# Layer 0's u table is split into half-precision parts ahead of the choosing stage and kept in DRAM

## The chip, the core and the metric

The kernel runs on one core of a Trainium2 chip. The core has a matrix engine (PE, with a separate weight load, PEld), a vector engine (DVE), a scalar engine (ACT), a general engine (POOL, which also issues the indirect DMAs), a queue engine that only issues DMAs (SP), and 16 DMA engines that all queues share. Each engine runs its own program in order; they meet only at semaphores. The metric is the device time of one execution in microseconds (us); lower is better.

## The reference

The reference is a two-layer block on 512 tokens of width 1024 with 256 context tokens beside them (768 tokens in six tiles of 128 in layer 0). Layer 0 mixes tokens with latent attention and a gated linear attention, layer 1 with a gated recurrence; behind each stands a product-key expert layer ("PEER"), on which this change bears:

```python
q = (ht @ wq).reshape(n_tok, 8, 256)
s1, s2 = q[..., :128] . k1, q[..., 128:] . k2        # 128 scores each
t1, i1 = top_k(s1, 16);  t2, i2 = top_k(s2, 16)      # best of both halves
top_s, pos = top_k(t1 + t2, 16);  idx = the 16 pairs # of 128 * 128 experts
g = softmax(top_s)
act = gelu(einsum('td,thkd->thk', hb, u[idx]))       # u: 16384 x 1024 a layer
out = einsum('thk,thkd->td', g * act, v[idx])
```

## The kernel before

**Stages.** The kernel is a chain of blocks with a barrier behind each: `modulation_vectors`, `modulate_columns`, `project_l0` (14 projections of 128 columns, then a value product V of six tiles), `latent_norms`, `attention` (48 softmax steps), twice `gla_decays`, `gla_states`, `gla_outputs`, then `gla_norm_gate`, `project_and_norm`; then PEER for layer 0: `peer_scores` (16 query projections with their scores), `choose_and_activate`, `combine_with_dots`. Layer 1 follows with its mixer and the same PEER functions.

**The choosing stage.** `choose_and_activate` does not gather u for most tokens. It takes the table in 128 chunks of 128 experts (512 KB each in float32) and multiplies each chunk with all tokens of `nt` tiles (four in layer 0, three in layer 1; the remaining tiles are gathered, below), writes the GELU of every product to DRAM (`acts`), and makes a one-hot gate matrix for each tile (`gates`). float32 is reached by halves: a chunk is split into a float16 high part `uh` and a float16 low part `ul = u - uh`, and each product is three float16 matmuls (line 1483), 24 a chunk in layer 0.

**Who splits a chunk before.** SP loads the chunk into one of four buffers `ur`. ACT casts it to `uh` (L1514). For an odd chunk DVE subtracts (L1577). For an even chunk ACT also writes the negated chunk (L1516) and POOL issues a DMA that adds `ur` to it (L1444). `LOW_BY` holds this table, the same for both layers. PE waits for the low part.

**Order in the stage.** `schedule` is the order all engines follow: `pre` chunks (12 in layer 0, 16 in layer 1), then for each tile a *choices part* (`ahead` chunks, 12 or 17, beside which DVE finds the top sixteen of a tile; PE then turns the result, L1492) and a *gates part* (`beside` chunks, 16 or 19, between 16 gate steps: DVE builds one-hot blocks, L1721 to L1725, and PE multiplies them, L1502). The tile's exponentials on ACT (L1535) stand behind chunk 7 (layer 0) or 10 (layer 1) of a choices part, and DVE waits for them at L1690. The gathered tiles cost DVE one dot product per chosen row (L1607, 256 in layer 0, 128 in layer 1). POOL fetches their rows by indirect DMA (L1457) into four buffers `ug`/`HS`, each fetch waiting for the dot product four back. In layer 0, 32 dot products stand behind each choice and 40 in each gates part; the low parts of the chunks stand between them in DVE's program, and the L1444 issues between the fetches in POOL's.

**Other places the change touches.** In `project_l0` POOL cuts each weight block into halves (L258, L259) when PE has finished the block two before, and ACT copies each product out of PSUM (L294), two products at a time in flight. `peer_scores` is built likewise (L1206, L1207, L1242), with a store of the scores per projection from ACT's queue (L1245).

Of the kernel before, what the change touches and what calls it, by code (L numbers as in the profile page):

```python
# [15 lines left out]
F32 = mybir.dt.float32  # L16
# [7 lines left out]
P = 128  # L24
D = 1024
# [195 lines left out]
def project_l0(nc, io, hh, hl, PT, V):  # L221

    with ExitStack() as c:
# [10 lines left out]
        with signals(nc, "wv_in", "wv_high", "wv_cut", "v_prod", "v_copied", "w_in0", "w_in1", "w_cut", "prod", "copied",  # L234
                     "pown", "w_high") as (wv_in, wv_high, wv_cut, v_prod, v_copied, w_in0, w_in1, w_cut, prod, copied, pown, w_high):
            w_in = (w_in0, w_in1)

            with nc.Block() as block:
                @block.sync
                def _(sp):  # L240
                    with sp.Fori(0, N_PROJ // 2) as it:
                        for j in range(2):
                            sp.wait_ge(w_cut, it * 2 + (j + 1))
                            sp.dma_start(w[j][:, :, :], io["ev_w_in"][bass.ds(it * 2 + j, 1)].rearrange("o p (k m) -> p (o k) m", k=KD)).then_inc(w_in[j], 16)
# [40 lines left out]
                def _(act):  # L285
# [5 lines left out]
                    with act.Fori(0, N_PROJ // 2) as it:  # L291
                        for j in range(2):
                            act.wait_ge(prod, it * 2 + (j + 3))
                            nc.scalar.activation(PT[:, bass.ds(it * 2 + j, 1), :].rearrange("p o t -> p (o t)"),  # L294
                                                 ps[j][:, 0:TOK], ACT.Copy).then_inc(copied, 1)

                @block.vector
                def _(dve):
                    for j in range(2):
                        dve.wait_ge(w_high, j + 1)  # L300
                        nc.vector.tensor_tensor(wl[j][:, :, :], w[j][:, :, :], wh[j][:, :, :], ALU.subtract).then_inc(w_cut, 1)
                    dve.wait_ge(wv_in, 16)
# [79 lines left out]
def attention(nc, io, PT, MIX, ident, halves):  # L382
# [4 lines left out]
    with ExitStack() as c:  # L387
# [7 lines left out]
        for x in halves:  # L395
# [12 lines left out]
                 "exped", "normed", "turned", "pt_copied", "av_done", "out_copied", "own")  # L408
        with signals(nc, *names) as (cs_in, wv_in, w_in0, w_in1, q_done, k_done, v_done, q_copied, k_copied, v_copied, roped, score, maxed,
# [1997 lines left out]
```

## Time and profile before

| | us |
|---|---|
| median of 3 runs (4462.70 to 4464.65) | 4462.87 |
| the profiled execution | 4453.52 |
| its span | 4451.7 |
| `project_l0` in it | 146.2 |
| `peer_scores`, layer 0 | 152.9 |
| `choose_and_activate`, layer 0 / layer 1 | 1002.9 / 703.1 |
| PE busy over the span | 84% |
| DVE busy over the span | 68% |

The profiled execution is 9.4 us under the median; stages are read from it alone. A busy share is an average over stages with different limits, and pipelined matmuls overlap in their records, so each stage is read by itself: its length, and the wait that ends last in it. "A <- B: t, n, m" in a list of waits means that A stood idle t us in n pieces, the longest m, until B released it.

### The profile page before, as it was taken

What the parts mean: (1) busy time and instruction counts of PE and PEld (TensorE: products, weight loads), DVE (VectorE), ACT (ScalarE), POOL (GpSimd) and SP (SyncE); (2) the same over time, 40 slices, a digit from 0 to 9 for tenths busy, and PEclk for the clock granted to TensorE, in tenths of its full rate; (3) what the DMA queues carried; (4) which work ended last, traced back from release to release, by engine and by line L of the source; (5) the groups of instructions that cost most, each with busy time, mean ns of one, the idle gap of its engine ahead of it and who ended that gap; (6) DMA issues with size and microseconds to landing.
All of it is one profiled execution on the core that took longest, in us unless ns stands there. A gap on an engine that the chain in (4) does not pass through costs nothing. (4 is left out here: it accounts for less than half of the span.)

```text
span 4451.7 us, 59762 instructions
## 1 busy us (share of the span) xinstructions
PE 3746.2 (84%) x19545; PEld 1934.9 (43%) x19545; DVE 3039.8 (68%) x6128; ACT 1447.7 (33%) x1842; POOL 1623.1 (36%) x1253
## 2 busy tenths in 40 slices
PE   6998778988959595969999978877998787699996
PEld 1555663643424242424444423434555454344442
DVE  2036445157968696859999976853578686588887
ACT  0115220023424242422332314841354444333332
POOL 0400000311434342437777731202223324277774
PEclk8989878999979897989999989988999998899998
DMA  5200250346989898989999982122699998899995
GB/s 209 76 28 1 78 152 9 98 140 188 344 292 338 298 346 296 325 339 403 404 404 403 404 307 77 59 88 69 192 257 346 286 329 284 314 330 347 341 346 220
DMA packets 397431, 1086.93 MB, mean 244 GB/s; under 512 B 38000, under 2 KB 124848, under 8 KB 390576
## 3 DMA queue, kind: packets, MB, share of 16 engines
q1 hardware_dynamic: 204380, 505.65, 31.1%
q0 software_dynamic: 128448, 435.22, 30.3%
q10 hardware_dynamic: 64420, 143.77, 8.7%
q8 instruction: 97, 1.59, 0.1%
q14 instruction: 86, 0.70, 0.0%
HBM read 921.87 MB, written 130.12 MB: 236 GB/s over the span
## 5 line engine op out<-in xcount | busy, mean ns | idle before, releaser
L1483 PE MATMUL ca_A<-hh,ca_uh 128*128 128x512 f16 (+1 forms) x2048 | 747.8, 365 | 270.8 <-DVE ca_ul L1577 196.6
L1483 PE MATMUL ca_A<-hl,ca_uh 128*128 128x512 f16 (+1 forms) x2048 | 745.8, 364 | 0.0
L1483 PE MATMUL ca_A<-hh,ca_ul 128*128 128x512 f16 (+1 forms) x2048 | 745.1, 364 | 0.0
L1913 PE MATMUL ex_R<-ex_vl,hh 128*128 128x512 f16 x1792 | 682.8, 381 | 0.0
L1913 PE MATMUL ex_R<-hl,hh 128*128 128x512 f16 x1792 | 542.3, 381 | 78.4 <-DVE hh L1927 58.0
L1944 DVE SCALAR_TENSOR_TENSOR ex_sum<-ex_vg,ex_share,ex_sum 128x1024 f32<-128x1024 f32 x384 | 493.1, 1284 | 9.8 <-DVE ex_share L1936 6.0
L1457 POOL DMA_INDIRECT ca_ug<-in_peer_u_rows,chosen_rows x288 | 296.4, 1029 | 458.4 <-DVE ca_ug L1607 403.7
L1841 POOL DMA_INDIRECT ex_vg<-in_peer_v_rows,ex_index x384 | 376.8, 981 | 193.1 <-DVE ex_ar L1922 86.5
L1607 DVE SCALAR_TENSOR_TENSOR ca_ug<-ca_ug,ca_hp 128x1024 f32<-128x1024 f32 x288 | 346.2, 1217 | 125.7 <-DMA ca_ug<-in_peer_u_rows,chosen_rows 124.0
L1483 PEld LDWEIGHTS ca_A<-hh,ca_uh 128*128 128x128 f16 x2048 | 205.9, 101 | 477.3 <-DVE ca_ul L1577 210.5
L1524 ACT ACTIVATE ca_ga<-ca_A 128x512 f32<-128x512 f32 (+1 forms) x256 | 139.2, 544 | 773.3 <-PE ca_A L1483 705.8
L1952 DVE TENSOR_TENSOR ACC<-ACC,ex_R 128x512 f32<-128x512 f32 x448 | 305.7, 682 | 110.8 <-PE ex_R L1913 107.5
L1913 PE MATMUL ex_R<-ex_vh,hh 128*128 128x512 f16 x896 | 341.4, 381 | 26.1 <-POOL ex_vl L1847 26.1
L1913 PE MATMUL ex_R<-ex_vh,ex_wl 128*128 128x512 f16 x896 | 341.0, 381 | 0.0
L1444 POOL DMA_DIRECT2D ca_ul<-ca_ur x124 | 118.8, 958 | 573.5 <-ACT ca_ul L1516 564.2
L1847 POOL TENSOR_TENSOR ex_vl<-ex_vr,ex_vh 128x1024 f16<-128x1024 f32 x128 | 268.5, 2130 | 118.1 <-PE ex_R L1913 75.7
L1913 PEld LDWEIGHTS ex_R<-hl,hh 128*128 128x128 f16 x1792 | 176.2, 98 | 299.1 <-issue 63.7
L1514 ACT ACTIVATE ca_uh<-ca_ur 128x1024 f16<-128x1024 f32 x248 | 261.1, 1053 | 129.3 <-ACT ca_ga L1524 45.2
L1483 PEld LDWEIGHTS ca_A<-hh,ca_ul 128*128 128x128 f16 x2048 | 206.0, 101 | 201.9 <-issue 24.9
L1483 PEld LDWEIGHTS ca_A<-hl,ca_uh 128*128 128x128 f16 x2048 | 206.1, 101 | 185.9 <-issue 22.5
L1847 POOL TENSOR_TENSOR ex_vl<-ex_vr,hl 128x1024 f16<-128x1024 f32 x120 | 251.8, 2131 | 86.5 <-PE ex_R L1913 78.6
L1913 PEld LDWEIGHTS ex_R<-ex_vl,hh 128*128 128x128 f16 x1792 | 176.1, 98 | 209.2 <-issue 3.5
(369 smaller groups left out, 6532.7 us busy)
## 6 DMA issues: line engine op xcount, KB each, us to landing
ca_ur<-in_peer_u SPq DMA_DIRECT2D x256, 512.0 KB, 6.5
ex_vr<-in_peer_v SPq DMA_DIRECT2D x256, 512.0 KB, 9.0
gates<-ca_stage ACTq DMA_DIRECT2D x28, 2048.0 KB, 12.7
acts<-ca_ga ACTq DMA_DIRECT2D x128, 256.0 KB, 5.2
ex_gr<-gates SPq DMA_DIRECT2D x32, 1024.0 KB, 10.8
ex_ar<-acts SPq DMA_DIRECT2D x128, 256.0 KB, 12.1
ca_ul<-ca_ur POOLq DMA_DIRECT2D x124, 256.0 KB, 7.7
acts<-ca_ga ACTq DMA_DIRECT2D x128, 192.0 KB, 5.7
```

The lines of the kernel that those rows point to most:

```text
L1444: nc.gpsimd.dma_start(ul[j][:, :, :].rearrange("p k n -> p (k n)"), ur[j][:, :, :].rearrange("p k n -> p (k n)"), accum_op=ALU.add).then_i ...
L1457: nc.gpsimd.indirect_dma_start(ug[x % UG][:, :], None, u_rows, bass.IndirectOffsetOnAxis(ap=chosen_rows[:, x:x + 1], axis=0)).then_inc(ug_ ...
L1483: last = nc.tensor.matmul(A[b][:, a:a + w], lhs[j][:, k, :], rhs[:, k, a:a + w], start=(k == 0 and x == 0), stop=(k == KD - 1 and x == 2))
L1514: nc.scalar.activation(uh[j][:, :, :], ur[j][:, :, :], ACT.Copy).then_inc(u_split, 1)
L1524: nc.scalar.activation(ga[b][:, :], A[b][:, 0:NT], ACT.Gelu).then_inc(gelu_done, 1)
L1607: nc.vector.scalar_tensor_tensor(ug[x % UG][:, :], ug[x % UG][:, :], 1.0, hp[:, :], ALU.mult, ALU.mult, accum_out=dots[:, x:x + 1]).then_i ...
L1841: nc.gpsimd.indirect_dma_start(ring[x][:, :], None, rows, bass.IndirectOffsetOnAxis(ap=index[q][:, x:x + 1], axis=0)).then_inc(done[x], 16)
L1847: nc.gpsimd.tensor_tensor(vl[q][:, x, :], vr[q][x][:, :], vh[q][:, x, :], ALU.subtract).then_inc(v_cut, 1)
L1913: last = nc.tensor.matmul(R[(NP * q + y) % BANKS][:, :], lhs[q][:, x, o:o + P], rhs[q][:, x, h * 512:h * 512 + 512], start=(x == 0 and n = ...
L1944: nc.vector.scalar_tensor_tensor(mine[:, :], vg[x][:, :], share[q][:, x:x + 1], mine[:, :], ALU.mult, ALU.add).then_inc(summed, 1)
L1952: nc.vector.tensor_tensor(part, part, R[(NP * q + y) % BANKS][:, :], ALU.add).then_inc(added, 1)
```

## The change

Layer 0's table is no longer split in the choosing stage. A helper `TableSplit` does it in six earlier blocks: SP loads a chunk into one of three `raw` buffers, ACT casts the high part into one of three `cut` buffers, DVE subtracts the low part beside it, and SP stores both (1024 float16 each per partition) to a DRAM tensor `u_parts`. `SPLIT_PROJECT` and the other tables give the places: 48 chunks in `project_l0` (2, then 3 beside each projection, then 1 beside each of four value tiles), 20 in `attention`, 6 in each `gla_outputs`, 7 in `project_and_norm`, 41 in `peer_scores` (3 beside each of 11 projections, 2 beside each of 4). In the choosing stage of layer 0 SP loads the finished halves, 512 KB a chunk as before, into a ring of eight; ACT casts nothing, DVE subtracts nothing there and POOL issues fetches only. Loops of SP and ACT in `project_l0`, and of SP, ACT and DVE in both layers' `peer_scores`, are written out.

`LOW_BY` changes for layer 1 too, which the short description does not say: the even chunks' low parts are subtracted by POOL itself instead of by its DMA, and ACT's negation (L1516) falls away.

The core of the diff:

```diff
+class TableSplit:
+    def load(self, sp, i):
+        r = i % len(self.raw)
+        if i >= len(self.raw):
+            sp.wait_ge(self.low_made, i - len(self.raw) + 1)
+        sp.dma_start(self.raw[r], self.table[self.first + i]).then_inc(self.raw_in[r], 16)
+    def store(self, sp, i):
+        b = i % len(self.cut)
+        sp.wait_ge(self.low_made, i + 1)
+        sp.dma_start(self.parts[self.first + i].rearrange("p x n -> p (x n)"), self.cut[b].rearrange("p x n -> p (x n)")).then_inc(self.stored[b], 16)
+    def move(self, sp, a, b, count):
+        for i in range(a, b):
+            self.store(sp, i)
+            if i + self.ahead < count:
+                self.load(sp, i + self.ahead)
+    def high(self, act, i):
+        act.wait_ge(self.raw_in[r], i // len(self.raw) * 16 + 16)
+        if i >= len(self.cut):
+            act.wait_ge(self.stored[b], i // len(self.cut) * 16)
+        self.nc.scalar.activation(self.cut[b][:, 0, :], self.raw[r], ACT.Copy).then_inc(self.high_made, 1)
+    def low(self, dve, i):
+        dve.wait_ge(self.high_made, i + 1)
+        self.nc.vector.tensor_tensor(self.cut[b][:, 1, :], self.raw[r], self.cut[b][:, 0, :], ALU.subtract).then_inc(self.low_made, 1)
...
+SPLIT_PROJECT = (2,) + (3,) * N_PROJ + (1,) * (TILES - 2)
+SPLIT_ATTENTION = 20
+SPLIT_SCORES = (3,) * 11 + (2,) * 4
...
 RING = 4
-LOW_BY = (("dma", "vector", "dma", "vector"), ("dma", "vector", "dma", "vector"))
+SPLIT_RING = 8
+LOW_BY = (None, ("gpsimd", "vector", "gpsimd", "vector"))
...
@@ choose_and_activate, SP
+                    if ready:
+                        with sp.Fori(1, PCH // SPLIT_RING) as k:
+                            for j in range(SPLIT_RING):
+                                sp.wait_ge(first_done, k * SPLIT_RING + (j + 1 + RING - SPLIT_RING))
+                                sp.dma_start(ring.us[j][:, :, :, :].rearrange("p x k n -> p (x k n)"),
+                                             parts[bass.ds(k * SPLIT_RING + j, 1)].rearrange("o p x n -> p (o x n)")).then_inc(u_in[j], 16)
+                        return
@@ choose_and_activate, PE
+                        if ready:
+                            j = (n * CT + x) % SPLIT_RING
+                            pe.wait_ge(u_in[j], (n * CT + x) // SPLIT_RING * 16 + 16)
+                            high, low = ring.us[j][:, 0, :, :], ring.us[j][:, 1, :, :]
```

How instructions move, at three places. First ACT in `project_l0`, from its value-weight load on; `PT` is the product copied out of PSUM, `pr_raw` and `pr_cut` are the split's buffers. Before (a loop of two copies):

```order
L290 DMA pwv<-in_ev_w_v 128x4096
L291 UNCONDITIONAL_BRANCH
L291 ISA
L294 ISA
L294 ACTIVATE PT<-pps 128x768
L293 REGISTER_ALU
```

Now:

```order
L366 DMA pwv<-in_ev_w_v 128x4096
L256 ACTIVATE pr_cut<-pr_raw 128x1024 x2
L370 ACTIVATE PT<-pps 128x768
L256 ACTIVATE pr_cut<-pr_raw 128x1024 x3
L370 ACTIVATE PT<-pps 128x768
L256 ACTIVATE pr_cut<-pr_raw 128x1024 x3
```

Three casts now stand behind every copy that frees a PSUM buffer for PE.

Second, DVE in layer 0's choosing stage, the last of a tile's 32 dot products and what follows (`ca_ug` and `HS` are the fetched rows, `ca_cols` begins the gates part). Before:

```order
L1577 TENSOR_TENSOR ca_ul<-ca_ur,ca_uh 128x1024
L1607 SCALAR_TENSOR_TENSOR ca_ug,dots<-ca_ug,ca_hp 128x1024 x3
L1607 SCALAR_TENSOR_TENSOR HS,dots<-HS,ca_hp 128x1024
L1607 SCALAR_TENSOR_TENSOR ca_ug,dots<-ca_ug,ca_hp 128x1024 x3
L1607 SCALAR_TENSOR_TENSOR HS,dots<-HS,ca_hp 128x1024
L1734 CAST ca_cols<-ca_G 128x384
L1736 TENSOR_TENSOR ca_cols<-ca_G,ca_cols 128x128
```

Now:

```order
L1788 SCALAR_TENSOR_TENSOR HS,dots<-HS,ca_hp 128x1024
L1788 SCALAR_TENSOR_TENSOR ca_ug,dots<-ca_ug,ca_hp 128x1024 x3
L1788 SCALAR_TENSOR_TENSOR HS,dots<-HS,ca_hp 128x1024
L1788 SCALAR_TENSOR_TENSOR ca_ug,dots<-ca_ug,ca_hp 128x1024 x3
L1788 SCALAR_TENSOR_TENSOR HS,dots<-HS,ca_hp 128x1024
L1915 CAST ca_cols<-ca_G 128x384
L1917 TENSOR_TENSOR ca_cols<-ca_G,ca_cols 128x128
```

The low parts, for which PE waited, are gone from between the dot products.

Third, POOL in layer 1's choosing stage, in its gates part. Before, a fragment:

```order
L1444 DMA ca_ul<-ca_ur 128x1024
L1457 DMA ca_ug<-in_peer_u_rows,chosen_rows 128x1024 x2
L1444 DMA ca_ul<-ca_ur 128x1024
L1457 DMA ca_ug<-in_peer_u_rows,chosen_rows 128x1024
L1457 DMA HS<-in_peer_u_rows,chosen_rows 128x1024
```

Now:

```order
L1615 TENSOR_TENSOR ca_ul<-ca_ur,ca_uh 128x1024
L1632 DMA ca_ug<-in_peer_u_rows,chosen_rows 128x1024 x2
L1615 TENSOR_TENSOR ca_ul<-ca_ur,ca_uh 128x1024
L1632 DMA ca_ug<-in_peer_u_rows,chosen_rows 128x1024
L1632 DMA HS<-in_peer_u_rows,chosen_rows 128x1024
```

POOL's order is the same; where it issued a DMA it now computes.

## Rows read from the trace of the kernel before

**Rows 1.** Windows by stage: PE, PEld, DVE, ACT, POOL busy, clock, DMA share, GB/s.
```profile
113.30:259.50 146.20, 141.91 (x816) 80.04 (x816) 16.27 (x12) 11.36 (x14) 52.26 (x24) 0.99 0.16 58
...
781.60:934.50 152.90, 148.06 (x961) 97.03 (x962) 23.88 (x25) 12.98 (x16) 56.26 (x28) 0.98 0.34 103
934.50:1937.40 1002.90, 766.52 (x4108) 366.80 (x4108) 781.52 (x2268) 350.63 (x407) 326.02 (x322) 0.89 0.88 294
1937.40:2633.40 696.00, 668.69 (x3072) 301.65 (x3072) 642.71 (x839) 201.21 (x253) 504.51 (x377) 0.98 1.00 388
...
3168.00:3871.10 703.10, 579.02 (x3850) 354.31 (x3851) 509.15 (x1473) 316.06 (x385) 195.18 (x193) 0.92 0.92 296
```

**Rows 2.** Waits in layer 0's choosing stage: us in total, times, longest.
```profile
PE ca_A L1483 <- DVE ca_ul L1577: 166.0, 14, 22.4
DVE ca_ug L1607 <- DMA ca_ug<-in_peer_u_rows,chosen_rows: 92.9, 74, 3.6
...
DVE ca_cols L1734 <- PE ca_G L1492: 15.5, 1, 15.5
```

**Rows 3.** Windows of parts, layer 0: first, gates, gates, choices.
```profile
934.50:1098.90 164.40, 131.98 (x576) 57.64 (x577) 127.92 (x719) 59.99 (x69) 15.00 (x16) 0.89 0.56 167
1104.50:1202.80 98.30, 94.67 (x618) 49.48 (x617) 89.57 (x144) 46.68 (x54) 46.85 (x45) 1.00 1.00 335
...
1330.00:1433.50 103.50, 97.04 (x616) 50.50 (x617) 90.87 (x145) 46.07 (x53) 47.30 (x45) 0.98 1.01 334
1433.50:1560.10 126.60, 73.23 (x319) 31.75 (x316) 90.78 (x317) 30.86 (x36) 39.37 (x41) 0.82 0.90 306
```

**Rows 4.** ACT timeline, start and us: the GELUs of two chunks in a row.
```profile
1088.83 0.60 ACT L1524 ACTIVATE ca_ga<-ca_A 128x512 f32<-128x512 f32 x1 [2.17 <-PE ca_A L1483]
...
1094.01 0.60 ACT L1524 ACTIVATE ca_ga<-ca_A 128x512 f32<-128x512 f32 x1 [3.11 <-PE ca_A L1483]
```

**Rows 5.** DVE timeline, the last of those windows: exponentials awaited, dot products over.
```profile
1488.11 0.29 DVE L1690 TENSOR_REDUCE ca_sm<-ca_ex 128x8 f32<-128x128 f32 x1 [8.94 <-ACT ca_ex L1535]
...
1556.45 0.55 DVE L1734 CAST ca_cols<-ca_G 128x384 f16<-128x384 f32 x1
```

**Rows 6.** Fetches of rows (line 1457, layer 0): issue to landing.
```profile
DMA to landing us min/median/max: 4.1/6.6/15.9
```

**Rows 7.** Groups by line: count, busy us, mean ns, idle before: cast, low, POOL's subtraction.
```profile
L1514 ACT ACTIVATE ca_uh<-ca_ur 128x1024 f16<-128x1024 f32 x248 | 261.1, 1053 | 129.3 <-ACT ca_ga L1524 45.2 <-issue 41.3 <-DMA ca_ur<-in_peer_u 39.6
...
L1577 DVE TENSOR_TENSOR ca_ul<-ca_ur,ca_uh 128x1024 f16<-128x1024 f32 x124 | 151.2, 1220 | 40.4 <-ACT ca_uh L1514 39.7 <-PE ca_A L1483 0.2 <-DVE chosen_gates L1693 0.2
...
L1207 POOL TENSOR_TENSOR sc_wl<-sc_w,sc_wh 128x1024 f16<-128x1024 f32 x28 | 59.5, 2126 | 2.2
```

**Rows 8.** Windows of layer 1: a gates part and a choices part.
```profile
3525.40:3616.30 90.90, 84.43 (x666) 55.59 (x665) 79.89 (x134) 49.14 (x59) 37.22 (x36) 0.96 1.02 337
3616.30:3736.50 120.20, 85.40 (x463) 47.69 (x461) 76.68 (x283) 41.00 (x50) 29.77 (x32) 0.84 0.88 291
```

**Rows 9.** Waits in layer 1's first choices part (3405 to 3511 us).
```profile
PE ca_A L1483 <- DMA ca_ul<-ca_ur: 30.6, 6, 14.6
```

**Rows 10.** ACT timeline in project_l0: one projection's copy, idle time before it.
```profile
178.08 0.81 ACT L294 ACTIVATE PT<-pps 128x768 f32 x1 [6.99 <-PE pps L271]
```

**Rows 11.** Timeline in project_l0, DVE and POOL side by side.
```profile
122.74 6.12 DVE L305 TENSOR_TENSOR pvl<-pwv,pvh 128x4096 f16<-128x4096 f32 x1
...
124.65 6.19 POOL L259 TENSOR_TENSOR pwl<-pw,pwh 128x1024 f16<-128x1024 f32 x1
```

**Rows 12.** ACT timeline in layer 0's peer_scores: a pair's first copy.
```profile
864.49 0.81 ACT L1242 ACTIVATE sc_qT<-sc_Q 128x768 f32<-128x768 f32 x1 [9.67 <-PE sc_Q L1220]
```

**Rows 13.** DMA queue of ACT in that stage: packets, MB, share of 16 engines.
```profile
q10 hardware_dynamic: 12544, 6.29, 16.2%
```

**Rows 14.** Waits in attention.
```profile
ACT at_p L533 <- DVE at_small L564: 55.4, 47, 3.1
```

**Rows 15.** DMA issues in layer 0's combine_with_dots: count, size, us to landing.
```profile
ex_vr<-in_peer_v SPq DMA_DIRECT2D x123, 512.0 KB, 12.9
```

More of the change, by code:

```diff
@@ L301, in _ @@
                         nc.vector.tensor_tensor(wl[j][:, :, :], w[j][:, :, :], wh[j][:, :, :], ALU.subtract).then_inc(w_cut, 1)
+                    for i in range(upto[4]):
+                        rows.low(dve, i)
                     dve.wait_ge(wv_in, 16)
@@ L308, in _ @@
                         nc.vector.tensor_copy(V[:, t, :], pv[t % 2][:, :]).then_inc(v_copied, 1)
+                        for i in groups[N_PROJ + 1 + t] if N_PROJ + 1 + t < len(groups) else ():
+                            rows.low(dve, i)
 def latent_norms(nc, io, PT, ones, ident):
@@ L777, in gla_outputs, with _ @@
         qe, ke, qs, S, sc = g["qe"], g["ke"], g["qs"], g["S"], g["sc"]
-        with signals(nc, "score", "kept", "out_done", "out_copied") as (score, kept, out_done, out_copied):
+        count = len(SPLIT_OUTPUTS)
+        with signals(nc, "score", "kept", "out_done", "out_copied") as (score, kept, out_done, out_copied), \
+                table_split(nc, io, parts, SPLIT_FIRST[2 + p], f"go{p}") as rows:
             with nc.Block() as block:
+                @block.sync
+                def _(sp):
+                    for i in range(rows.ahead):
+                        rows.load(sp, i)
+                    rows.move(sp, 0, count, count)
+                    rows.all_stored(sp, count)
                 @block.tensor
@@ L1160, in table_ring, with split_ring, peer_scores @@
                    LOW_BY[layer])
-def peer_scores(nc, io, hh, hl, scores, layer, first_tile, ring):
+@contextmanager
+def split_ring(nc, layer):
+    with ExitStack() as c:
+        us = [c.enter_context(nc.sbuf_tensor(f"ca_us{b}{layer}", [P, 2, KD, P], F16)) for b in range(SPLIT_RING)]
+        yield SplitRing(us, c.enter_context(signals(nc, *[f"u_in{b}" for b in range(SPLIT_RING)])))
+def peer_scores(nc, io, hh, hl, scores, layer, first_tile, ring, parts):
     N = 2 * PH
@@ L1285, with choose_and_activate @@
 PRE = (12, 16)
-def choose_and_activate(nc, io, ident, hh, hl, scores, gates, acts, chosen_rows, chosen_gates, layer, first_tile, kept, u_rows, dots, ring):
+def choose_and_activate(nc, io, ident, hh, hl, scores, gates, acts, chosen_rows, chosen_gates, layer, first_tile, kept, u_rows, dots, ring, parts):
     c0 = first_tile * P
```

197 lines of the change are left out of this document (150 added, 47 removed).

## Prediction

> **What bounds the kernel now.** I read first the windows by stage, since the change takes work out of one stage and puts it into six others. In layer 0's choosing stage (1002.9 us) PE is busy 766.5 and DVE 781.5: neither fills it, and PE's clock is granted at 0.89 of full speed, a sign of idle stretches [rows 1]. `project_l0` and `peer_scores`, which take 89 of the 128 chunks, are the reverse: PE is busy 141.9 of 146.2 and 148.1 of 152.9, DVE, ACT and DMA nearly idle (DMA share 0.16 and 0.34) [rows 1].
>
> Next I read the waits of the choosing stage. PE stood 166 us for the low part that DVE makes; DVE itself waited 93 us for fetched rows [rows 2]. Then the stage in parts. Each gates part (four, 98.3 to 103.5 us) is nearly full of PE work; each choices part (three, 126.6 to 127.5) has only 73 us of it; and the first part is 164.4 long [rows 3]. PE needs 5.18 us a chunk when nothing stops it, the distance of two GELUs [rows 4].
>
> **The change: layer 0's choosing stage.**
> *First part.* 24 chunks at 5.18 are 124.3 us. DVE was through 15.5 us before PE [rows 2], so PE was last, held up by low parts queued behind DVE's three choices. Freed, it ends at about 127. DVE is next: of its 127.9 busy us [rows 3], ten low parts at 1.22 [rows 7] go, leaving 115.7, and about 14 of its waits at the start and for scores stay: 130. Gain 34; bounds 24 (no wait of DVE shrinks) and 37 (PE's floor).
>
> *Choices parts.* Here DVE is the chain. In the one that I follow PE starts at 1433.5 and DVE has chosen at 1488.11 - 8.94 = 1479.2, and then waits for exponentials that stand behind PE's eighth chunk [rows 5]. Unhindered, that chunk ends at 1433.5 + 8 x 5.18 = 1474.9, the exponentials about 3 later, and DVE, rid of two low parts, is there at 1476.8: dot products begin at 1479 instead of 1489, gain 10. They then ran until 1556.45 [rows 5]: 67.5 us, less two low parts (2.4) and a copy (1.2), is 2.0 us each for 32, against 1.22 that one takes. Four fetches are in flight, and a median landing of 6.6 plus 1.4 for the dot product and the new issue, over 4, is that 2.0 [rows 6]. The added transfers and the chunk loads disappear from these us (eight chunks are held ahead), so I take a landing near the shortest, 4.1, giving 1.5: 16 gained, and 2.4 for the low parts. In all 28 a part; bounds 12 (the fetches stay as slow) and 32 (1.4 each). Three parts: 84.
>
> *Gates parts.* PE's own busy 95 to 97 is the floor of 98 to 104 [rows 3]; eight low parts (9.8 us) leave DVE's 90. Gain 5 each, bounds 0 and 8: 20.
> Sum: 34 + 84 + 20 = **138 less**.
>
> **Layer 1's choosing stage.** A choices part is 120.2 us with 85 us of PE work [rows 8]; PE waits 30.6 of it for low parts that arrive through POOL's DMA [rows 9]. POOL now subtracts in 2.13 us [rows 7], and ACT's negation, the issue and a transfer go. But POOL's place in the order stays: a low part still stands behind fetches, which stand behind dot products, so not all comes back: 28 a part, bounds 15 and 33, two parts: 56. A gates part (90.9) is PE-bound already, busy 84.4 [rows 8]; POOL's subtraction beside DVE's can only cost, 4 each for three (bounds 0 and 12): 12. The first part (134.4 us) I leave alone. Sum: **44 less**.
>
> **What the splitting costs.** *Projection.* PE has a period of 6.99 + 0.81 = 7.80 us [rows 10]. Beside it there are now three loads, three stores and a weight block, seven transfers of 512 KB. The best sustained rate, DMA share 1.00, was 388 GB/s in `combine_with_dots` [rows 1], 1.35 us each: 9.45. ACT holds PE's buffers behind casts that wait for those loads, so PE takes that pace: 1.65 x 13 = 21. DVE's and POOL's subtractions may not overlap: one on POOL took 6.19 beside one of 6.12 on DVE [rows 11], against 2.13 alone; 4 more, so 25. Bounds: 12 if the DMA does a little better, 45 if a ring round (landing about 6.5, cast 1.05, low 1.22, issues 0.7) cannot be kept full.
>
> The Trainium skill (DMA: Bandwidth & Descriptors, Specifications) gives a limit of about 358 GB/s of HBM traffic for one core, which would make seven transfers 10.25 us and this term 32 instead of 21. The trace disagrees: 388 was held for 696 us.
>
> *Scores.* A pair of projections takes 9.67 + 0.81 + 7.80 = 18.28 us [rows 10, 12]. ACT's queue used 16.2% of 152.9 for 16 stores, 1.55 each [rows 13]. A pair then needs 12 transfers and 2 weight blocks at 1.35 and two stores: 22.0. That is 3.7 more for 5.5 pairs: 20 (bounds 10 and 40). The groups of two at the end fit in. *Attention.* ACT waits 55.4 us for DVE in 48 steps, 1.15 each [rows 14], which covers its casts of 1.05; DVE's 20 low parts fit into its own shorter waits only partly, 0.4 each: 8 (0 to 20). *The two output blocks* of 25 us take six chunks each, two rounds of the ring: 4 each, 8 (0 to 15). *Norm:* 3 (0 to 6). Sum: **64 more**, between 22 and 126.
>
> **Sum.** -138 - 44 + 64 = -118 on the profiled execution of 4453.5: 4335.5. The median of the runs is 9.4 higher, so I forecast 4345. Everything else, `combine_with_dots` above all (DMA share 1.00 [rows 1]), I keep.
>
> **Rivals.**
> *A. The fetches stay the bound of the dot products.* Their landing of 6.6 may come from their own four in flight rather than from the other traffic. Then choices gain 12, not 28: 48 less gain, 4393. For it: DVE waited for fetches in every part. Against: the shortest landing is 4.1.
>
> *B. POOL's subtraction and DVE exclude each other in layer 1.* Rows 11 show the pattern. In a gates part, 9.5 of them at 2.13 would add 20 us to DVE's 79.9, past the 90.9: 12 more with waits, three times, and half of the 56 goes. Layer 1 then loses 8 and the total is -66: 4397. Against it: a dot product is another form of instruction, and no row here shows that form held up. The Trainium skill (SBUF — State Buffer, Who interferes with whom) says that a DVE instruction with two SBUF inputs and a POOL instruction that reads SBUF share one port, held for a whole instruction; by that rule, dot products count too.
>
> *C. The splitting is paced by its ring of three, and the kernel is slower.* Under a full DMA queue a 512 KB load took 12.9 us to land [rows 15]. A round for three chunks is then 12.9 + 1.05 + 1.22 + 0.7 = 15.9, against 7.80 and 9.14: 8.1 x 13 + 6.8 x 11 = 180, and 19 for the other places. Less the 182 gained that is 17 more: 4480. It decides from a landing of about 12.2. Against it: only three loads are in flight here, and `combine_with_dots` keeps more.
>
> *D. The splitting is nearly free:* stores overlap loads and the DMA keeps 7.8 a group. Cost 30, not 64: 4311.
>
> That the change does not do what it says I set aside: ACT's casts and DVE's low parts are absent from layer 0's stage in the order of instructions.
>
> **How the numbers follow.** Forecast 0.55, A 0.14, B 0.11, C 0.07, D 0.13. A, B and D lie between 4311 and 4397; with the bounds of the unknown terms, mostly dot products (48), projection and scores (-23, +40), and layer 1 (-20, +50), the range is 4265 to 4425, leaving out C and the outer tails, under 0.2. About 0.2% (9 us) is what a measurement of this kernel tells from no change. Faster by more: 0.92, within it 0.01, slower 0.07.
>
> **What would show it.** In the changed profile: PE no longer waits for a low part in layer 0; the first part is near 130 and a choices part near 98, with the dot products 1.5 us apart (2.0 would be A). In layer 1, choices near 92 and gates near 95 (103 would be B). `project_l0` near 171 and `peer_scores` near 173, ACT waiting there for raw loads, DMA share near 0.9 (rounds of 16 us would be C, stages of unchanged length D). I am wrong if PE's wait in the choices parts merely moves to the one-hot blocks behind unchanged dot products, or if the two projection stages grow by over 100.

## The result and the profile after

The changed kernel takes 4389.18 us (median of 4 runs, 4382.94 to 4394.67) against 4463.76 of the kernel before in the same rounds (4 runs, 4462.70 to 4470.08): ratio 0.983, 95% interval 0.9813 to 0.9847. It is faster by 1.7%, clear of the scatter and inside the range, but by 74.6 us and not by the 118 that I had forecast. The profiled execution is 4389.7 with a span of 4387.9, against 4453.5 and 4451.7 before: 63.8 us less of span, where my sum said 118. (The profiled execution of before lay 9.4 under its median; that of after lies at its own. So the steps below are compared by the profiled executions.)

Windows by stage, as in [rows 1]: `project_l0`, layer 0's `peer_scores`, its `choose_and_activate` and `combine_with_dots`, and layer 1's `choose_and_activate`. The columns are the stretch, its length, busy us of PE, PEld, DVE, ACT and POOL with instruction counts, the granted clock, the DMA share and GB/s.

```profile
113.50:289.40 175.90, 150.81 (x816) 81.41 (x816) 87.88 (x60) 60.51 (x62) 60.54 (x24) 0.93 0.87 331
823.10:998.80 175.70, 154.85 (x961) 98.34 (x962) 66.27 (x58) 54.50 (x58) 63.59 (x28) 0.93 0.93 343
998.80:1901.60 902.80, 734.10 (x4109) 364.61 (x4110) 712.72 (x2206) 168.74 (x221) 257.94 (x260) 0.90 0.86 306
1901.60:2599.80 698.20, 669.16 (x3072) 300.39 (x3072) 640.71 (x840) 201.75 (x253) 519.23 (x377) 0.98 1.00 387
3132.20:3809.30 677.10, 571.44 (x3849) 352.39 (x3850) 570.70 (x1473) 257.79 (x323) 266.54 (x193) 0.93 0.79 283
```

The stages that split have become 29.7 and 22.8 us longer, with the DMA share up from 0.16 and 0.34 to 0.87 and 0.93. Layer 0's choosing stage is 100.1 shorter and layer 1's 26.0. `combine_with_dots`, which I had left alone, grew by 2.2.

By part, in us. A choices part is measured here from the GELU of the last chunk ahead of it to PE's first one-hot product, a gates part from there to the GELU of its last chunk, in both kernels alike:

| part | before | after | change | forecast |
|---|---|---|---|---|
| layer 0: start to the first one-hot product | 170.0 | 134.7 | -35.3 | -34 |
| four gates parts | 400.1 | 374.2 | -25.9 | -20 |
| three choices parts | 383.4 | 343.2 | -40.2 | -84 |
| end of the stage | 49.5 | 50.6 | +1.1 | 0 |
| layer 1: two choices parts | 241.8 | 211.4 | -30.4 | -56 |
| three gates parts | 265.6 | 266.6 | +1.0 | +12 |
| its start and end | 195.7 | 199.2 | +3.5 | 0 |
| `project_l0` | 146.2 | 175.9 | +29.7 | +25 |
| `peer_scores`, layer 0 | 152.9 | 175.7 | +22.8 | +20 |
| `attention` | 193.0 | 198.5 | +5.5 | +8 |
| both `gla_outputs` | 51.2 | 60.0 | +8.8 | +8 |
| `project_and_norm`, layer 0's first | 116.6 | 117.3 | +0.7 | +3 |

From the program's start to layer 0's choosing stage the splitting costs 64.3 us in all (934.5 to 998.8), where my sum said 64. What failed is the choosing stages: 38 us are missing in layer 0 and 18 in layer 1.

The waits in layer 0's choosing stage, as in [rows 2] (total us, times, longest):

```profile
PE ca_G L1683 <- DVE ca_hot L1906: 137.6, 3, 46.8
DVE ca_ug L1788 <- DMA ca_ug<-in_peer_u_rows,chosen_rows: 87.0, 81, 3.8
```

PE's 166 us of waiting for low parts are gone. In their place PE stands in three pieces of 46 us, one in each choices part, until DVE makes the first one-hot block; and DVE still waits for fetched rows about as long as before: 87 us against 93 for the rows in `ca_ug`, 113 against 116.5 with those in `HS`. The prediction had named this as a sign of being wrong: PE's wait has moved to the one-hot blocks, behind dot products that have hardly changed.

The parts that answer [rows 3] (first part, two gates parts, a choices part):

```profile
998.80:1128.00 129.20, 127.18 (x577) 56.94 (x578) 116.39 (x709) 24.67 (x34) 3.90 (x4) 0.98 0.58 182
1133.50:1226.10 92.60, 92.60 (x617) 50.12 (x616) 83.35 (x142) 24.94 (x31) 40.10 (x39) 1.00 0.96 343
1340.40:1435.30 94.90, 94.89 (x617) 51.12 (x618) 83.58 (x138) 24.38 (x30) 38.00 (x37) 0.97 0.92 325
1435.30:1549.90 114.60, 67.78 (x318) 30.75 (x314) 83.29 (x309) 11.66 (x17) 32.77 (x35) 0.81 0.91 336
```

The first part is 129.2 long (I had said 130), a gates part is all PE work (busy 92.6 of 92.6). A choices part holds 67.8 us of PE work in 114.6. DVE's timeline in that part, the counterpart of [rows 5] (start, us, instruction, and in brackets the idle time before it and what ended it):

```profile
1479.79 0.28 DVE L1871 TENSOR_REDUCE ca_sm<-ca_ex 128x8 f32<-128x128 f32 x1 [4.36 <-ACT ca_ex L1716]
...
1545.12 1.22 DVE L1788 SCALAR_TENSOR_TENSOR HS<-HS,ca_hp 128x1024 f32<-128x1024 f32 x1 [0.72 <-DMA HS<-in_peer_u_rows,chosen_rows]
...
1546.26 0.55 DVE L1915 CAST ca_cols<-ca_G 128x384 f16<-128x384 f32 x1
```

The exponentials are there 44.5 us into the part, against 54.6 before: the 10 us that I had said. But the 32 dot products behind them still need 65.5 us, 2.05 each, against 67.5.

### The profile page after: what moved, and what is told of

Its sections match the earlier page's. It is cut to its first block and busy times, and to the rows that moved or that the text cites. A ratio compares the mean times of both kernels' runs of the same rounds, so it can differ in the third digit from the quotient of the medians.

```text
span 4387.9 us, 59379 instructions
## 1 busy us (share of the span) xinstructions
PE 3720.1 (85%) x19545; PEld 1931.6 (44%) x19545; DVE 3190.3 (73%) x6186; ACT 1333.8 (30%) x1722; POOL 1656.8 (38%) x1191
## 5 line engine op out<-in xcount | busy, mean ns | idle before, releaser
L1664 PE MATMUL ca_A<-hh,ca_us 128*128 128x512 f16 x2048 | 625.8, 382 | 13.5 <-ACTq L1731 11.5
L1632 POOL DMA_INDIRECT ca_ug<-in_peer_u_rows,chosen_rows x288 | 286.1, 994 | 718.8 <-DVE ca_ug L1788 596.3
L2022 POOL DMA_INDIRECT ex_vg<-in_peer_v_rows,ex_index x384 | 391.3, 1019 | 204.2 <-DVE ex_ar L2103 97.7
L1664 PE MATMUL ca_A<-hh,ca_uh 128*128 128x384 f16 x1024 | 343.8, 336 | 76.2 <-DVE ca_ul L1758 54.1
L1664 PE MATMUL ca_A<-hl,ca_us 128*128 128x512 f16 x1024 | 391.1, 382 | 0.0
L1664 PE MATMUL ca_A<-hl,ca_uh 128*128 128x384 f16 x1024 | 343.4, 335 | 0.0
L1664 PE MATMUL ca_A<-hh,ca_ul 128*128 128x384 f16 x1024 | 343.0, 335 | 0.0
L1664 PEld LDWEIGHTS ca_A<-hh,ca_us 128*128 128x128 f16 x2048 | 201.6, 98 | 251.6 <-issue 21.0
L1683 PE MATMUL ca_G<-ca_hot 128*128 128x128 f16 x896 | 117.7, 222 | 140.1 <-DVE ca_hot L1906 140.1
L2057 ACT ACTIVATE hh<-ex_ar 128x512 f16<-128x512 f32 (+1 forms) x256 | 141.7, 576 | 278.5 <-DVE ex_ar L2103 278.4
```

Source lines behind the costliest of these rows:

```text
L1632: nc.gpsimd.indirect_dma_start(ug[x % UG][:, :], None, u_rows, bass.IndirectOffsetOnAxis(ap=chosen_rows[:, x:x + 1], axis=0)).then_inc(ug_ ...
L1664: last = nc.tensor.matmul(A[b][:, a:a + w], lhs[:, k, :], rhs[:, k, a:a + w], start=(k == 0 and x == 0), stop=(k == KD - 1 and x == 2))
L1683: last = nc.tensor.matmul(G[j][:, x, :], one(part), one(0), start=(part == 1), stop=(part == 2))
L2022: nc.gpsimd.indirect_dma_start(ring[x][:, :], None, rows, bass.IndirectOffsetOnAxis(ap=index[q][:, x:x + 1], axis=0)).then_inc(done[x], 16)
L2057: nc.scalar.activation(wh[q][:, x, :], ar[x][:, :], ACT.Copy).then_inc(w_high, 1)
```

## The experiments

Where nothing in a stage was changed, most stages repeat within about 2 us between these profiles. Four scatter more: `project_l0` (174.0 to 178.5), layer 0's `peer_scores` (173.0 to 178.8) and its choosing stage (898.5 to 904.8), and layer 1's single choices parts (104 to 113; the pair of them 211 to 217). Where one time is given, it is one execution, to be read beside 4389.

**Layer 1's table alone.** The change has two independent parts. This run undoes one:

```diff
-LOW_BY = (None, ("gpsimd", "vector", "gpsimd", "vector"))
+LOW_BY = (None, ("dma", "vector", "dma", "vector"))
```

> The changed kernel with layer 1's low parts of even chunks made as before (POOL's adding DMA, ACT's negation); layer 0 keeps its split table. It tells the two parts of the change apart. If layer 1's gain of 26 us comes from that table alone, its choosing stage returns from 677 to about 703 us, a choices part from 106 to 121, a gates part stays at 88 to 90, and the time rises by 26 to about 4415; layer 0's choosing stage stays at 903. Rival: layer 1 gains from something else (what layer 0 leaves behind, noise): its stage stays within 8 us of 677.

Measured: 4411.0 us, layer 1's choosing stage 700.5, its choices parts 117.3 and 117.0, gates parts 87.6 to 91.6; layer 0's stage 901.4. So 22 of the 75 us come from the table for layer 1, which the short description of the change does not name, and about 53 from layer 0's split.

**What holds the fetched rows: other traffic, or their own number.** My step said that landings near 4.1 us would return once other transfers are gone. Here the chunk loads are all but taken away. This kernel leaves out fifteen sixteenths of each chunk after the first eight, so its products mean nothing and only its times do:

```diff
-sp.dma_start(ring.us[j][:, :, :, :].rearrange("p x k n -> p (x k n)"),
-             parts[bass.ds(k * SPLIT_RING + j, 1)].rearrange("o p x n -> p (o x n)")).then_inc(u_in[j], 16)
+sp.dma_start(ring.us[j][:, :, 0, 0:64],
+             parts[bass.ds(k * SPLIT_RING + j, 1), :, :, 0:64].rearrange("o p x n -> p (o x) n")).then_inc(u_in[j], 16)
```

> The changed kernel, but in layer 0's choosing stage only a sixteenth of each chunk's halves is loaded after the first eight chunks, so the products there are of stale halves. It takes almost all chunk traffic away from the fetched rows. Theory W (my prediction's: other transfers slow the fetches): their landing falls from 5.4 to near 4.1 us, dot products come 1.5 us apart instead of 2.03, a choices part falls from 114 to about 98, the stage by 45 or more. Theory A (four fetches in flight set their own pace): dot products stay 1.9 to 2.05 apart, choices parts at 110 to 115, the stage within 15 us of 903.

Measured: 4381.55 us; choices parts 112.1, 113.0 and 110.0 (115.0, 115.4 and 112.8 in the changed kernel), the stage 893.4, dot products 1.90 to 2.00 apart. In one stretch of 32 dot products the chunk loads of the changed kernel and of this run are:

```profile
ca_us<-u_parts SPq DMA_DIRECT2D x5, 512.0 KB, 7.4
```

```profile
ca_us<-u_parts SPq DMA_DIRECT2D x5, 32.0 KB, 5.1
```

The fetches' time to landing in that stretch of this run:

```profile
DMA to landing us min/median/max: 4.8/5.5/8.0
```

And the window of that stretch (columns as in the stages above):

```profile
1270.80:1334.00 63.20, 23.30 (x110) 10.56 (x108) 39.77 (x68) 4.27 (x6) 29.03 (x31) 0.71 0.83 280
```

The landing in the same stretch of the changed kernel:

```profile
DMA to landing us min/median/max: 4.7/5.6/9.2
```

And its window:

```profile
1270.60:1336.80 66.20, 23.33 (x110) 10.61 (x108) 39.68 (x68) 4.27 (x6) 29.03 (x31) 0.71 0.88 314
```

With almost no chunk traffic, a landing is 5.5 instead of 5.6 us. Theory W falls: the chunk loads were not what the fetches waited for. A landing counts from the start of POOL's issue. From the end of a dot product to the start of the fetch into its buffer lie 0.82 us (the median of this stretch), and the dot product takes 1.22. So a buffer's round is about 5.5 + 0.8 + 1.2 = 7.5 us, with four buffers 1.9 us a row, close to what the run shows. (The expectations put 1.24 for the 0.82. That is POOL's step from one fetch to the next, and 0.94 of it lies in the landing already.)

**Eight rows in flight.** They need room that the ring of eight chunks takes. So a control first, with the shorter ring alone:

```diff
-SPLIT_RING = 8
+SPLIT_RING = 4
```

> The changed kernel with a ring of four chunks of finished halves instead of eight in layer 0's choosing stage. It is the control for the next run, which needs the room. If the depth of the ring hardly matters (a chunk lands in 6.4 us and PE takes 5.2 to 6.1 a chunk), the stage stays within 8 us of 903. If eight were needed to bridge bursts of fetches and gate stores, PE waits for chunks and the stage grows by 20 to 60.

Measured: 4378.34 us, layer 0's choosing stage 898.5, `peer_scores` 169.0: the ring's depth is not needed in the choosing stage. Then the test itself:

```diff
-    UG = 4
+    UG = 8 if ready else 4
```

> Ring of four chunks, and eight instead of four buffers for fetched rows in layer 0. If the wait for a landing with only four in flight sets the pace (theory A, latency: 5.4 + 1.24 + 1.22 over 4 = 1.97), eight in flight bring dot products to the issue rate of about 1.3 us, a choices part falls by about 23 to 91 to 95 and the stage by 70 against the ring of four. If the DMA engines are the bound (their share was 0.89 to 0.93 in these stretches, a fetched packet took 182 ns), landings grow instead, dot products come about 1.8 apart, a choices part falls by 7 and the stage by 20. If neither, nothing moves.

Measured: 4338.01 us, the stage 851.8, choices parts 99.4, 99.6 and 96.6, dot products 1.56, 1.56 and 1.47 apart. The landing in the same stretch of this run:

```profile
DMA to landing us min/median/max: 6.5/8.2/17.2
```

And its window:

```profile
1268.90:1319.40 50.50, 23.31 (x110) 10.58 (x108) 39.27 (x68) 4.27 (x6) 28.53 (x31) 0.76 0.96 376
```

The number in flight was the bound: with eight, the same 32 rows take 50.5 us instead of 66.2. Neither extreme came: at POOL's issue rate it would be 1.3 us a row, but landings grew from 5.6 to 8.2 and the DMA share to 0.96. That the transfers' rate holds next is likely from that share, but no run tests it. Here 29 us a choices part are won against before, the size that I had forecast, but by another means. Timed in rounds:

> Ring of four and eight fetch buffers alone, timed in rounds beside the kernel before: 4338 within 6, ratio about 0.972, against 0.983 of the changed kernel as given.

Measured: 4340.18 us (4 runs, 4334.44 to 4343.15), ratio 0.9726, interval 0.9705 to 0.9747.

**The exponentials two chunks earlier**, on top of that:

```diff
-    ahead, beside, midway_at = {4: (12, 16, 7), 3: (17, 19, 10)}[nt]
+    ahead, beside, midway_at = {4: (12, 16, 5), 3: (17, 19, 10)}[nt]
```

> The kernel with ring four and eight fetch buffers, and layer 0's exponentials on ACT behind the sixth chunk of a choices part instead of the eighth. DVE has chosen 38 us after the part's start and then waits about 6 us until the exponentials of 44.9 come. If that wait is on the path, dot products begin 5 to 6 us earlier, each of three choices parts falls from 98.5 to about 93, layer 0's choosing stage by 16 to 18 to about 835. If the dot products are then held by landings again, or PE's own 12 chunks (62 us) and the one-hot blocks set the end, it falls by less than 4.

Measured: 4332.21 us, the stage 849.8, only 2 us less. Its parts say why: dot products begin 10.4 us earlier (34.9 into the part), come 1.72 us apart instead of 1.53, and choices parts fall by 4.4 each to 94.2; but the first part, which the number also governs, grew by 11 (144.6 after 133.6). Both theories were half right. The start moved by 10 and not by 6 because DVE had waited longer than the 6 us of the expectation: in the run with eight buffers and the old place it waited for the exponentials three times, 11.8 us in each of these parts, and here 1.4 to 1.5.

```profile
DVE ca_sm L1871 <- ACT ca_ex L1716: 35.4, 3, 11.8
```

**Splitting elsewhere.** The price of 64 us was forecast by the DMA's rate in each group of chunks. If so, it depends on where the chunks stand:

```diff
-SPLIT_PROJECT = (2,) + (3,) * N_PROJ + (1,) * (TILES - 2)
-SPLIT_ATTENTION = 20
-SPLIT_SCORES = (3,) * 11 + (2,) * 4
+SPLIT_PROJECT = (2,) + (2,) * N_PROJ
+SPLIT_ATTENTION = 46
+SPLIT_SCORES = (2,) * 15 + (3,)
```

> The changed kernel with the chunks split elsewhere: 30 in the first projections instead of 48 (two beside each), 46 in attention instead of 20, 33 in the scores instead of 41. Theory by the rate of the DMA (my sum: a transfer costs 1.35 us, a group pays only what exceeds PE's 7.8 us): two chunks and a weight block are 6.75, so the projection falls from 176 to 154 to 158 (the stop of about 10 us beside DVE's value weights stays), the scores from 176 to 157 to 162, attention rises at its 0.27 us a chunk from 198 to 206: 28 less in all. Rival by the ring (each chunk costs its round whatever the group): costs go by the count, the projection 165, the scores 171, and attention, where DVE works 1.2 us more in each step, rises by 15 or more: no gain in all.

Measured: 4373.42 us. The windows of `project_l0` and `peer_scores` in this run:

```profile
113.00:263.20 150.20, 143.67 (x817) 80.19 (x817) 74.41 (x42) 40.58 (x44) 62.74 (x24) 0.98 0.72 262
813.99:983.55 169.56, 148.79 (x960) 96.90 (x961) 59.34 (x50) 45.42 (x50) 62.62 (x28) 0.93 0.88 305
```

Two chunks beside a projection cost next to nothing: `project_l0` is 150.2, and most copies are 7.80 us apart again. By the count of chunks it would have been 165. So the rate theory holds there, and was too dear for two: the group of five transfers fits under PE's 7.8 us. Attention rose by 15.4 to 213.9, twice what I had said: 0.59 us for each further chunk, not the 0.27 of the first twenty. In `peer_scores` the projections ran as before the change (copies 136.0 us from first to last, as in the kernel before), yet the stage was 169.6: its end, from the last copy on, took 23.4 us against 14.1 in the changed kernel and 7.4 before. Behind the last chunk's store SP issues eight loads for the next stage and then waits until all stores have landed, and the barrier waits for SP; which of these weighs most was not told apart here. (In the run with a ring of four, so four loads, the end took 9.0 us: the four further loads are 5 of the changed kernel's 14.1.) In the changed kernel PE's timeline shows the smaller form of that stop:

```profile
998.75 0.58 PE L1664 MATMUL ca_A<-hh,ca_us 128*128 128x512 f16 x1 [11.48 <-ACTq L1731]
```

**The stop in the projections.** In the changed kernel one projection took 19.2 us where the others took 8.1 to 10.4. DVE's timeline ahead of it, and then ACT's:

```profile
151.25 3.99 DVE L382 CAST pvh<-pwv 128x4096 f16<-128x4096 f32 x1
155.27 6.22 DVE L384 TENSOR_TENSOR pvl<-pwv,pvh 128x4096 f16<-128x4096 f32 x1
```

```profile
168.96 1.06 ACT L256 ACTIVATE pr_cut<-pr_raw 128x1024 f16<-128x1024 f32 x1 [9.40 <-DMA pr_raw<-in_peer_u]
```

For 10.2 us DVE makes no low part, so no buffer of the ring of three comes free, nothing is loaded, and ACT's next cast comes 9.4 us late. What PE itself waits for is a weight block: SP issues its load behind the stores and loads of the chunks, and POOL halves it when it has landed. From 130 to 260 us this is PE's only wait in the list, and its longest piece, 8.6, is the stop:

```profile
PE pps L347 <- POOL pwl L335: 18.0, 6, 8.6
POOL pwh L334 <- DMA pw<-in_ev_w_in: 52.7, 11, 12.1
```

With the value weights split in eight pieces, two low parts of chunks ahead of each piece's subtraction and one behind it:

```diff
-nc.vector.tensor_copy(vh[:, :, :], wv[:, :, :]).then_inc(wv_high, 1)
-dve.wait_ge(wv_high, 1)
-nc.vector.tensor_tensor(vl[:, :, :], wv[:, :, :], vh[:, :, :], ALU.subtract).then_inc(wv_cut, 1)
+for k in range(KD):
+    nc.vector.tensor_copy(vh[:, k, :], wv[:, k, :]).then_inc(wv_high, 1)
...
+    dve.wait_ge(wv_high, k + 1)
+    nc.vector.tensor_tensor(vl[:, k, :], wv[:, k, :], vh[:, k, :], ALU.subtract).then_inc(wv_cut, 1)
...
```

> The changed kernel, but DVE splits the value weights of the first projections in eight pieces with chunk low parts between, instead of 10.2 us in one stretch in which no low part is made. In the trace PE stood still for 8.6 us behind that stretch and one projection took 19.2 instead of 9.4. If DVE's stretch is what stopped the ring of three, the projection stage falls from 176 to 166 to 168. If the stop has another source (POOL beside DVE, the value weights' own load of 2 MB), it stays within 3 us of 176.

Measured: 4387.12 us, `project_l0` 168.4, 7.5 less; no projection took over 10.4 us. DVE's long stretch was the stop. (The whole is only 2 us less: the stages behind came out 5 us longer in sum, which is within their scatter.)

**Layer 1: who subtracts.** There the choices parts came to 105.7 and not to my 92.

```diff
-LOW_BY = (None, ("gpsimd", "vector", "gpsimd", "vector"))
+LOW_BY = (None, ("vector", "vector", "vector", "vector"))
```

> The changed kernel with all of layer 1's low parts on DVE and none on POOL. In the changed kernel DVE's one-hot blocks were stretched by 51 us in all where POOL subtracted, but layer 1's gates parts stayed at 88 to 89. If that stretch is what keeps its choices parts at 106 instead of my 92 (rival B there: first one-hot block 5.1 instead of 0.7), a choices part falls by 3 to 6. If DVE is the chain there and POOL's help is worth more than the stretch costs, eight or nine more low parts of 1.22 make a choices part 5 to 10 longer, and gates parts 0 to 5, and the stage grows by 15 to 30.

Measured: 4396.21 us, layer 1's choosing stage 676.8 (677.1), choices parts 108.6 and 111.5, all three gates parts 86.5. Neither forecast: what the gates parts win (2.4 each), the choices parts lose (4.4 each; about 3.4 against the mean of all runs that leave layer 1 as it is). POOL's help and POOL's harm are of one size.

**Layer 1: rows in flight.** The room allows five buffers; three was run for the other direction (`UG = 4 if ready else 5`, and `3`).

> The changed kernel with five instead of four buffers for fetched rows in layer 1 alone. There a choices part stayed at 105 to 106 where I had said 92; its 16 dot products come 2.06 us apart (with low parts between) and landings are 6.7 us. If the number of fetches in flight holds them there too ((6.7 + 1.24 + 1.22) over 5 = 1.83 instead of 2.29 a row as far as rows wait), a choices part falls by 3 to 6. If the low parts, their casts on ACT and POOL's place in the order hold it, it stays within 2 of 105.7.

> The same with three buffers. If the fetches hold layer 1's choices parts, (6.7 + 1.24 + 1.22) over 3 = 3.05 a row makes each 10 to 13 longer than 105.7, and gates parts, which have 16 rows' time and more to spare, 0 to 4 longer. If they don't, a choices part grows by less than 4.

Measured: with five 4388.59 us, choices parts 103.9 and 106.3, landings 7.7 instead of 6.7; with three 4433.26 us, choices parts 119.4 and 115.9, gates parts 92.5 to 97.8, the stage 716.5. Three hold the part, and four are enough there: a fifth only waits longer. So in layer 1 the fetches are not what is left.

**Together.** Ring of four, eight buffers, the exponentials earlier in the later parts only, and the chunks spread, with none beside the last projection of the scores:

```diff
-                        if x == midway_at:
+                        if x == midway_at - (2 if ready and last is not None else 0):
...
+SPLIT_SCORES = (3,) * 3 + (2,) * 12
```

> What the runs so far point to, together: ring of four, eight fetch buffers, exponentials two chunks earlier in the three choices parts that follow a gates part (the first part keeps its place, since the earlier run lost 11 us there), and the split of 30 chunks in the projections, 46 in attention, 33 in the scores, with none beside the last of the score projections, where the stage's end had grown from 14 to 23 us. From 4338: projection -26, attention +15, scores -12 to -16, choosing -13: about 4300. Rival: the parts are not independent (the clock of PE, which the records show granted lower in denser stages, and the DMA near its full share in the choices parts) and half of that is lost: 4315 to 4325.

Measured: 4300.34 us (5 runs, 4299.65 to 4303.65), ratio to the kernel before 0.9644, interval 0.9626 to 0.9661: better than both kernels, 89 us under the changed one. Windows of `project_l0`, `attention`, `peer_scores` and layer 0's choosing stage in it:

```profile
113.40:262.70 149.30, 142.44 (x817) 80.02 (x817) 74.35 (x42) 41.08 (x44) 61.66 (x24) 0.99 0.72 263
285.40:495.80 210.40, 176.19 (x1018) 105.63 (x1018) 157.77 (x295) 129.28 (x213) 4.66 (x5) 0.92 0.67 242
811.90:974.50 162.60, 151.70 (x961) 97.76 (x962) 59.69 (x50) 45.65 (x50) 61.69 (x28) 0.95 0.88 305
974.50:1812.80 838.30, 733.37 (x4108) 364.56 (x4109) 709.18 (x2206) 168.76 (x221) 252.79 (x260) 0.94 0.90 333
```

Against the run with eight buffers that is -25.8, +12.3, -9.8 and -13.5: the parts add up. The splitting now costs 40 us (934.5 to 974.5) instead of 64.

## Why the prediction was half right

**Direction and price of the splitting: right, the sum partly by luck.** The forecast was 64 us and 64.3 were measured, term by term within 5. The mechanism was the DMA's rate. Behind the stop, the changed kernel's projections kept the DMA engines full:

```profile
185.00:240.00 55.00, 48.59 (x285) 27.82 (x283) 24.53 (x18) 22.16 (x23) 28.57 (x12) 0.97 1.01 389
```

The copies of products there (178 to 235 us) come 9.45 us apart on average, the length of seven transfers in my sum, and two chunks a projection instead of three took the cost away. A round of the ring of three would be nearly as long (a landing of 6.0 with the cast, low part and issues of my bound is 9.0); it is the full share that speaks for the rate, and a deeper ring was not run. The path was another than I had it: PE did not wait for copies that ACT held back, but for weight blocks queued behind the chunks. And the close sum is partly luck: of the projections' 29.7, 10 were the stop beside the value weights, and of the scores' 22.8, 7 were the stage's end. No term of mine names either. The pace itself cost about 18 and 16, less than my 21 and 20. The Trainium skill (DMA: Bandwidth & Descriptors, Specifications) gives 358 GB/s as one core's limit of HBM traffic; by it, as an estimate, the projections' term would have been 32. The trace does not agree: 389 GB/s in the row above, and 387 held in the changed kernel's `combine_with_dots` for 698 us, so the figure is no ceiling here. In the term of 25 I had put 4 for POOL and DVE excluding each other, after [rows 11]; the larger thing was DVE's own 10.2 us in front of a ring of three.

**The first part and the gates parts: right** (-35.3 for -34, -25.9 for -20). The reasoning held: PE's own work is the floor, and it is now reached.

**The dot products in layer 0's choices parts: wrong, and rival A was right.** The step was "I take a landing near the shortest, 4.1, giving 1.5: 16 gained". The start moved by the 10 us that I had worked out, but the pace stayed at 2.05 us: the choices parts gained 13.4 each instead of 28, 44 of the 54 us that my sum is off by. A's figure was 12. (That the time itself lies so near A's 4393 is partly luck: A kept layer 1's 44, of which 26 came.) The error is in reading [rows 6]: the median of 6.6 is one of the whole stage, in which gates parts with their stores and chunk loads lie too. In the stretch that mattered, the dot products of the choices part that the prediction follows, the landing was already shorter. This is the row that should have been asked for:

```profile
DMA to landing us min/median/max: 4.2/6.0/9.2
```

The sum that seemed to confirm the reading fitted by luck: 6.6 + 1.4 is 8.0, but in that stretch it was 6.0 to land and 2.0 for the rest (0.82 from a dot product's end to the next fetch, 1.22 for the dot product). Its window (1488.1 to 1556.4 us) had few chunk loads, four, for PE stood still and the ring was full. So there was little of that traffic to take away; leaving out nearly all chunk loads moved the landing to 5.5 and no further, while eight in flight moved the pace to 1.5. (Stores of activations and gates stayed in that run; what they alone add was not tried.) The shortest of 4.1 was a landing that few fetches have, not what an undisturbed one takes behind three others.

**Layer 1: the mechanism right, the size wrong.** Its choices parts lost 15.2 us each, not 28 (the lower bound that I had given was 15). The 30.6 us for which PE waited in the first of them [rows 9] are gone, and the exponentials are there 8.6 us earlier (52.8 us into the part instead of 61.4). But PE now waits there for the low parts that DVE and POOL make. First DVE's share before, then both after:

```profile
PE ca_A L1483 <- DVE ca_ul L1577: 5.6, 2, 4.8
```

```profile
PE ca_A L1664 <- DVE ca_ul L1758: 15.6, 4, 9.3
PE ca_A L1664 <- POOL ca_ul L1615: 8.2, 2, 7.5
```

So PE's waits for low parts fell from 36.2 to 23.8 us only. The longest piece of POOL's, 7.5 (8.3 in the second choices part), is the caution of the prediction come true: the subtraction stands behind fetches, and the first of these waited 17 us for a dot product.

```profile
3426.71 0.95 POOL L1632 DMA_INDIRECT ca_ug<-in_peer_u_rows,chosen_rows  x1 [16.99 <-DVE ca_ug L1788]
...
3432.32 2.13 POOL L1615 TENSOR_TENSOR ca_ul<-ca_ur,ca_uh 128x1024 f16<-128x1024 f32 x1
```

The longest piece of DVE's, 9.3 instead of 4.8, is rival B at a place where I had not looked. Two of POOL's subtractions fall on DVE's first instruction for the one-hot blocks, which takes 5.11 us instead of 0.69, and the low part for which PE waits comes behind it:

```profile
3458.16 5.11 DVE L1902 TENSOR_TENSOR hh<-ca_iota,ca_cols 128x1024 f16<-128x1024 f16 x1
...
3466.39 0.50 PE L1664 MATMUL ca_A<-hh,ca_uh 128*128 128x384 f16 x1 [9.25 <-DVE ca_ul L1758]
```

PE's first one-hot product then comes 19.8 us behind DVE's cast of the turned choice (L1915), where it came 14.1 behind the same cast (L1734) before. With POOL's DMA (14.3 and 13.9) or DVE's own subtraction (14.3 and 14.4) the loss is absent, so this is shown: 4.4 of the 5.7 us are the stretch itself. The other 1.3 fall into the two chunks behind it, which took 10.6 us at a granted clock of 0.73 instead of 9.3 at 0.84. What can be won of the rest stays open: five buffers gained nothing beyond the scatter, and with all low parts on DVE PE waited 25.8 us for them in this part, so the wait only moved.

**Rival B itself is there, and was cheap.** The one-hot block's last product (two float16 inputs in SBUF), in layer 1's stage of the changed kernel and then in the run with POOL's DMA (ns, min/median/max):

```profile
L1906 DVE TENSOR_TENSOR ca_hot<-hh,ca_cols x48: 691/693/2899, 3268.7 to 3759.2; 128x1024 f16<-128x1024 f16 x48
```

```profile
L1906 DVE TENSOR_TENSOR ca_hot<-hh,ca_cols x48: 691/692/703, 3269.6 to 3778.8; 128x1024 f16<-128x1024 f16 x48
```

Over the stage, lines 1902 and 1906 were stretched by 51 us. Yet the gates parts grew by 1.0 in all instead of 12, because DVE had 11 us to spare in each (busy 79.9 of 90.9 in [rows 8]): its busy time rose to 87.8 of 89.4 us. It was not free, for without POOL's subtractions a gates part is 2.4 shorter. The answer to [rows 8]:

```profile
3477.00:3566.40 89.40, 83.83 (x653) 55.05 (x651) 87.76 (x119) 40.01 (x49) 45.65 (x35) 0.96 0.85 295
3566.40:3671.60 105.20, 82.63 (x475) 47.44 (x473) 86.67 (x297) 32.99 (x42) 41.69 (x32) 0.89 0.85 317
```

**Rivals C and D.** The loads landed in 6.0 and 6.5 us at the median, not in 12.9 and far from the 12.2 at which C would decide, so C fell. D (30 us) was no property of the change as given, but the runs with two chunks a projection come near it for that stage: 4 us instead of 29.7.

## What to carry to other kernels

Where a consumer waits for a stream of fetches, work out (landing + issue + use) over the number in flight from the stretch itself, before giving the wait to other traffic: if it is close to the pace seen, more in flight is what helps. Here the room came from a ring that was deeper than it had to be, and the eight rows brought 47 us in that stage (898.5 to 851.8). Work moved into "idle" engines is paid by the group, at the DMA's rate and against the length of the step that it stands beside: two chunks beside 7.8 us were nearly free (4 us in the stage), three were not, and one long instruction ahead of a short ring stops everything behind it. When a wait goes, name the next one with its own row.

## What the runs showed of the hardware that I had not expected

A DVE instruction that falls together with a POOL subtraction is held or not by its operands. POOL and DVE side by side in a gates part of layer 1, first POOL, then DVE:

```profile
3532.55 2.13 POOL L1615 TENSOR_TENSOR ca_ul<-ca_ur,ca_uh 128x1024 f16<-128x1024 f32 x1 [1.44 <-ACT ca_uh L1695]
...
3542.62 2.14 POOL L1615 TENSOR_TENSOR ca_ul<-ca_ur,ca_uh 128x1024 f16<-128x1024 f32 x1
```

```profile
3532.69 1.22 DVE L1788 SCALAR_TENSOR_TENSOR ca_ug<-ca_ug,ca_hp 128x1024 f32<-128x1024 f32 x1
...
3533.83 1.40 DVE L1902 TENSOR_TENSOR hh<-ca_iota,ca_cols 128x1024 f16<-128x1024 f16 x1
...
3542.42 2.90 DVE L1906 TENSOR_TENSOR ca_hot<-hh,ca_cols 128x1024 f16<-128x1024 f16 x1
```

The dot product inside POOL's 3532.55 to 3534.68 takes its usual 1.22; the one-hot product takes until 0.55 us after POOL's end, and the later one 2.90 instead of 0.69. All 21 dot products of that stage that overlap a POOL subtraction by over 0.3 us took 1.21 to 1.22. One of the dot product's two inputs (`ca_hp`) lies in PSUM; both of the one-hot's lie in SBUF. Nor is it the form of the instruction: in `combine_with_dots` a TENSOR_TENSOR with one input in PSUM (`ex_R`) runs beside POOL's subtractions, 93 times with an overlap of over 0.3 us, and is never stretched (ns, min/median/max):

```profile
L2133 DVE TENSOR_TENSOR ACC<-ACC,ex_R x256: 675/679/689, 1906.4 to 2577.9; 128x512 f32<-128x512 f32 x128
```

The Trainium skill (SBUF — State Buffer, Who interferes with whom) says that a DVE instruction with at most one input in SBUF, outside the two-port modes, does not contend with POOL, and that one with two such inputs contends with a POOL instruction that reads SBUF. The trace agrees, and by that rule, read rightly, the dot products do not count, against what I wrote in rival B.

Splitting lowered the granted clock where it made PE wait: 0.99 in `project_l0` before, 0.93 with three chunks a projection, 0.98 to 0.99 with two. These are means of a clock that is granted at 1.2 or 2.4 GHz. The same 816 matmuls were busy 141.9, 150.8 and 142 to 144 us. So some 9 of those 29.7 us were slower matmuls at the lower clock, and not the wait itself.
